# Router logits with tokens on the partitions: the normed rows as stationary operand, eight output columns, four PSUM banks

## The reference

```python
def moe_swiglu(x, w_router, w_gu, w_down):
    logits = jnp.einsum('bsd,de->bse', x, w_router).astype(jnp.float32)
    top_val, top_idx = lax.top_k(logits, TOP_K)
    gates = jax.nn.softmax(top_val, axis=-1)
    ...
    for e in range(N_EXPERTS):
        out = out + gate_full[..., e:e + 1] * swiglu(x, w_gu[e], w_down[e])
```

## Time and profile before

| what | value |
|---|---|
| median of 3 runs | 1290.58 us (1287.37 to 1291.31) |
| the profiled execution | 1289.33 us |
| its span, first to last instruction | 1287.5 us |
| PE busy | 1231.6 us, 96% of the span |
| DVE busy | 657.5 us, 51% |
| ACT busy | 538.9 us, 42% |
| mean granted PE clock | 0.987 of full speed |
| DMA | 174.10 MB, mean 135 GB/s |

### The profile page before, as it was taken

One profiled execution on the slowest core, in us unless ns is written; L12 is line 12 of the kernel. 1 busy time (PEld: TensorE's weight loads), 2 busy tenths in 40 slices (PEclk: granted clock), 3 DMA queues, 4 the chain that ended last, 5 costly groups with the idle time before them and its releaser, 6 DMA issues.

```text
span 1287.5 us, 16720 instructions
## 1 busy us (share of the span) xinstructions
PE 1231.6 (96%) x6081; PEld 1030.7 (80%) x6082; DVE 657.5 (51%) x863; ACT 538.9 (42%) x723; POOL 55.7 (4%) x67
## 2 busy tenths in 40 slices
PE   7999999999999999999999999999979999999678
PEld 6889998688888888888688789987668788877567
DVE  5333454743333333333763345534676676677774
ACT  3225541453222232213532223422576666676642
POOL 1000000000000000000000000000001312121000
PEclk9999999999999999999999999999989999999979
DMA  7331112323333333333135644122399796799751
GB/s 198 96 94 58 50 50 77 103 82 98 98 98 98 98 115 114 90 90 94 40 112 85 63 98 60 41 83 72 107 322 303 232 347 219 235 321 320 272 225 51
DMA packets 199013, 174.10 MB, mean 135 GB/s; under 512 B 7600, under 2 KB 163312, under 8 KB 198960
## 3 DMA queue, kind: packets, MB, share of 16 engines
q1 hardware_dynamic: 195264, 160.01, 42.9%
q0 software_dynamic: 3120, 11.27, 2.3%
q10 hardware_dynamic: 576, 2.10, 0.4%
HBM read 164.19 MB, written 9.18 MB: 135 GB/s over the span
## 4 chain that ended last, share of the span: by engine, by line
PE 86%; DVE 5%; DMA 3%; issue 3%; ACT 2%; ACTq 0%; SPq 0%; POOLq 0%; DVEq 0%
PE bank L792 26%; PE bank L793 25%; PE bank L794 25%; DMA raw<-moe_w_down 2%; PE bank L1184 2%; PE bank L1183 2%; DVE w_lo L1829 2%; DVE x_exact L1829 1%; PE bank L1159 1%; PE bank L1225 1%; ACT w_hi L1682 1%; PE bank L1111 1%; PE bank L885 0%; PE bank L970 0%; PE bank L930 0%
## 5 line engine op out<-in xcount | busy, mean ns | idle before, releaser
L1829 DVE TENSOR_TENSOR w_lo<-raw,w_hi 128x1024 fp32r<-128x1024 f32 (+4 forms) x206 | 285.5, 1396 | 167.4 <-ACT w_hi L1364 118.4
L792 PE MATMUL bank<-x_hi,w_hi 128*128 128x512 f32 x600 | 235.2, 392 | 3.5 <-DVE w_lo L1829 3.3
L793 PE MATMUL bank<-x_lo,w_hi 128*128 128x512 f32 x600 | 234.0, 390 | 0.0
L794 PE MATMUL bank<-x_hi,w_lo 128*128 128x512 f32 x600 | 233.9, 390 | 0.0
L1364 ACT CAST w_hi<-raw 128x1024 fp32r<-128x1024 f32 (+2 forms) x131 | 141.2, 1078 | 202.0 <-PE bank L794 202.0
L792 PE MATMUL bank<-w_hi,x_hi 128*128 128x256 f32 (+2 forms) x448 | 147.6, 329 | 7.6 <-DVE w_lo L1829 3.9
L793 PE MATMUL bank<-w_lo,x_hi 128*128 128x256 f32 (+2 forms) x448 | 145.1, 324 | 0.0
L794 PE MATMUL bank<-w_hi,x_lo 128*128 128x256 f32 (+2 forms) x448 | 144.9, 323 | 0.0
L792 PEld LDWEIGHTS bank<-x_hi,w_hi 128*128 128x128 f32 x600 | 113.0, 188 | 28.4 <-DVE w_lo L1829 4.4
L794 PEld LDWEIGHTS bank<-x_hi,w_lo 128*128 128x128 f32 x600 | 112.9, 188 | 23.7
L793 PEld LDWEIGHTS bank<-x_lo,w_hi 128*128 128x128 f32 x600 | 113.1, 188 | 23.0
(11 more groups left out here) (375 smaller groups left out, 2007.9 us busy)
## 6 DMA issues: line engine op xcount, KB each, us to landing
raw<-ffn_w_gu SPq DMA_DIRECT2D x44, 512.0 KB, 3.8
raw<-moe_w_gu SPq DMA_DIRECT2D x24, 768.0 KB, 8.5
raw<-a_w_qkv SPq DMA_DIRECT2D x24, 512.0 KB, 3.7
raw<-moe_w_gu SPq DMA_DIRECT2D x32, 384.0 KB, 6.5
raw<-moe_w_down SPq DMA_DIRECT2D x16, 768.0 KB
raw<-ffn_w_down SPq DMA_DIRECT2D x16, 704.0 KB, 4.4
raw<-kvf_w SPq DMA_DIRECT2D x16, 512.0 KB, 5.5
ring<-moe_w_down SPq DMA_DIRECT2D x16, 512.0 KB, 7.8
```

What stands on the lines that cost most here:

```text
L792: pe.matmul(o, s_hi, m_hi, start=start, stop=False, skip_group_check=True)
L793: pe.matmul(o, s_hi, m_lo, start=False, stop=False, skip_group_check=True)
L794: return pe.matmul(o, s_lo, m_hi, start=False, stop=stop, skip_group_check=True)
L1829: return dve.tensor_tensor(dst, a, b, ALU.subtract)
```

## The change

The operands of the router's matmul change places. For each k and each of the four token tiles t, a block of 128 tokens of `x_exact` (128 x 128) is the stationary operand and `w_r[:, k, :]` (8 columns) moves. The four results, 128 tokens x 8 experts each, lie in banks 4 to 7. They need no transpose: DVE copies each to its place in `logits`. The tile `logits_e`, its copy, the four transposes and the semaphore `logits_turned` go. `route_step` counts two more, and those who wait for it are adjusted.

```diff
-        logits_e = at("logits_e", [NE, SEQ], F32, G + 94 * KB)
...
             for k in range(KD):
                 pe.wait_ge(affine, 2 * KD + k + 1)
-                mm = pe.matmul(bank[5][0:NE, :], w_r[:, k, :], x_exact[:, k, :], start=k == 0, stop=k == KD - 1)
+                for t in range(TT):
+                    mm = pe.matmul(bank[4 + t][:, 0:NE], x_exact[:, k, t * P:(t + 1) * P], w_r[:, k, :],
+                                   start=k == 0, stop=k == KD - 1)
             mm.then_inc(router_done, 1)
...
-            pe.wait_ge(route_step, 1)
-            for t in range(TT):
-                mm = pe.transpose(bank[6][:, t * NE:(t + 1) * NE], logits_e[:, t * P:(t + 1) * P], ident[0:NE, 0:NE])
-            mm.then_inc(logits_turned, 1)
             turn_rows(0)
             turn_rows(1)
 
-            pe.wait_ge(route_step, 8)
+            pe.wait_ge(route_step, 10)
...
-            act.wait_ge(route_step, 4)
+            act.wait_ge(route_step, 6)
...
             dve.wait_ge(router_done, 1)
-            dve.tensor_copy(logits_e[:, :], bank[5][0:NE, :]).then_inc(route_step, 1)
-            dve.wait_ge(logits_turned, 1)
-            dve.tensor_copy(logits[:, :, :], bank[6][:, 0:TT * NE].rearrange("p (t e) -> p t e", e=NE)).then_inc(route_step, 1)
-            dve.wait_ge(route_step, 2)
             for t in range(TT):
+                dve.tensor_copy(logits[:, t, :], bank[4 + t][:, 0:NE]).then_inc(route_step, 1)
+            for t in range(TT):
+                dve.wait_ge(route_step, t + 1)
                 op = dve.max(top[:, t, :], logits[:, t, :])
             op.then_inc(route_step, 1)
```

More of the change, by code:

```diff
@@ L461, in build @@
         router_done = sem("router_done")
-        logits_turned = sem("logits_turned")
         route_step = sem("route_step")
@@ L2174, in _ @@
             dve.wait_ge(router_done, 1)
-            dve.tensor_copy(logits_e[:, :], bank[5][0:NE, :]).then_inc(route_step, 1)
-            dve.wait_ge(logits_turned, 1)
-            dve.tensor_copy(logits[:, :, :], bank[6][:, 0:TT * NE].rearrange("p (t e) -> p t e", e=NE)).then_inc(route_step, 1)
-            dve.wait_ge(route_step, 2)
             for t in range(TT):
+                dve.tensor_copy(logits[:, t, :], bank[4 + t][:, 0:NE]).then_inc(route_step, 1)
+            for t in range(TT):
+                dve.wait_ge(route_step, t + 1)
                 op = dve.max(top[:, t, :], logits[:, t, :])
             op.then_inc(route_step, 1)
-            dve.wait_ge(route_step, 3)
+            dve.wait_ge(route_step, 5)
             minus(g_diff[:, :], top[:, :, 1], top[:, :, 0]).then_inc(route_step, 1)
@@ L2186, in _ @@
             op.then_inc(route_step, 1)
-            dve.wait_ge(route_step, 5)
+            dve.wait_ge(route_step, 7)
             dve.tensor_copy(top_f[:, :, :], top_at[:, :, 0:2]).then_inc(route_step, 1)
-            dve.wait_ge(route_step, 6)
+            dve.wait_ge(route_step, 8)
             for c in range(2):
@@ L2193, in _ @@
             op.then_inc(route_step, 1)
-            dve.wait_ge(route_step, 7)
+            dve.wait_ge(route_step, 9)
             dve.tensor_tensor(sel_any[:, 0:TT, :], sel[:, 0, :, :], sel[:, 1, :, :], ALU.add).then_inc(route_step, 1)
```

## The result

| | before | after |
|---|---|---|
| median | 1286.85 us (20 runs) | 1290.01 us (20 runs) |
| range | 1284.23 to 1291.6 | 1286.22 to 1293.45 |
| span of the profiled execution | 1287.5 us | 1287.1 us |

The ratio is 1.0021, with a 95% interval of 1.0012 to 1.0031: by it the changed kernel is 2.7 us slower (1.5 to 4.0; the medians differ by 3.2), which is clear of no change but under the 0.3% that I had taken as the border. The two profiled spans do not show the loss at all. The reason comes further down: what follows the first expert's weight transfer varies by 4 us between executions, whatever the kernel. What the change does must be read from its own stretch.

The account below looks back on a forecast made before the run. PE was taken as the bound, busy 1231.6 of 1287.5 us. A list 2.1 us late gave 1291.4 from the profiled execution's 1289.33, or 1292.7 from the median; forecast 1292.0, range 1288.0 to 1297.5.

Parts of the forecast that it names:

- The router at full clock: Router matmuls on PE: 64 records at 0.117 us, 7.5 us plus 0.25 for the last result, 0.7 us longer than before.
- The handover: From the router's logits to MAX8 on DVE: four copies out of PSUM, 0.45 us against 1.43, 0.98 us saved.
- The clock falls in the router: PE's clock goes to half about 3.6 us into the router, records then 0.213 us apart; router ends at 920.1.
- The row transposes off the thread: PE's row transposes after the router start earlier and end long before DVE's sel_any, so they delay nothing.
- The sum: From router to end of list: counts 3.9 us late at 925.65, list at 931.9, so 2.1 us late.
- The clock back by the counts, DVE sets the list: After the counting matmuls: full clock on PE again, DVE's 5.64 us of tables set the list at 931.9; chance 0.45.
- The slow rival: Half clock from router to list: row transposes, embed_rows(1) and list cost 3.9 to 7.8 us, 1293.2 to 1298.4; chance 0.24.
- Do transposes count for the clock?: Row transposes on PE, 920.1 to 923.5: taken to bring the clock back; if not, time near the upper end, 7.8 us late.
- The rival of the swallowed delay: At the first expert, its 12.53 us wait for a weight transfer hides the late start: 1290.6 us; chance 0.06.

Follow-up runs that it names:

- 128-column run: Changed kernel with w_r streamed 16 times over, so each router matmul moves 128 columns and not 8: 0.9993 of the kernel before, median 1285.8 us.
- first profile with 64 columns: Changed kernel with w_r streamed 8 times over, so each router matmul moves 64 columns; first of two profiles: ratio 0.9991 to the kernel before.
- run with a known delay: Kernel before with three idle 512-column matmuls on PE ahead of the router: ratio 1.0018, 2.3 us slower (0.9 to 3.7).
- kernels with the clock kept: Changed kernel with 64 router columns (0.9991 of the kernel before), with 128 (0.9993), and with 128 plus five idle matmuls before the counts (0.9990).
- 8 and 32: Router columns per matmul: 8 is the changed kernel (1.0021 of the kernel before), 32 is it with w_r streamed 4 times over (1.0019).

## Why the prediction was right, and where it was not

- **The router at full clock: right.** 7.5 us from 0.117 for each record and 0.25 for the last result make 7.75; the 128-column run shows 7.43 with its result. No profile has the 8-column router at full clock to its end, but its records before the fall start about as far apart, (914.0 - 909.6) / 39 = 0.11 us.
- **The handover: right.** 0.45 us was forecast; 0.34 (919.31 to 919.65) and 0.40 (916.82 to 917.22) were measured. Router and handover together take 917.22 - 909.39 = 7.83 us with 128 columns, against 917.70 - 909.22 = 8.48 before. So at full clock the idea gains 0.65 us in the profiles and not 0.3.
- **The clock falls in the router: right.** Forecast 3.6 us in, seen 4.6 and 2.1 us in. The router's records at half clock in the second profile (shortest, median and longest in ns, first and last start):

```profile
L1110 PE MATMUL bank<-w_r,x_exact x46: 292/361/363, 911.5 to 921.0; 128*128 128x8 f32 x46
```

They start (921.0 - 911.5) / 45 = 0.21 us apart, for which I had taken 0.213: the load-bound spacing follows the clock in full. Columns / 1.2 ns, which the Trainium skill ("TensorE: Matmul & The Clock Gate", "LDWEIGHTS (loading the stationary operand)") gives for a load without regard to the clock, would be 0.107; the trace comes near it at full clock only.
- **The row transposes off the thread: wrong.** The prediction let them end long before `sel_any`. At half clock they take 3.51 us, in both profiles they stand in the chain, and in the first PE reaches the counts 0.2 us after `sel_any` (922.61 against 922.39). The sum was at odds with itself here: it had PE at the transposes until 923.5 and at the counts from 923.35.
- **The clock back by the counts, DVE sets the list: the step that failed** in the first profile. The row transposes between router and counts (919.2 to 922.6) did not bring the clock back; it came at 927.9, 3.1 us after the counts. PE then set the list again, 932.72 - 924.75 = 7.97 us after the counts, where I had 6.25. What made up for it was a shorter router (9.67 against 10.9). In the second profile the router took longer than forecast (11.93), but the clock was back by 925.2, and the list followed the counts by 932.48 - 926.10 = 6.38 us, as forecast. Both routes end in the same place, 23.1 us, against the 22.7 of the sum. The slow rival's mechanism was thus half there, its price was not. That the sum came so near in the first profile is two errors that cancel.
- **Do transposes count for the clock?** The Trainium skill, on the same page ("Part 4: PE-mode transpose"), holds that they do not. The traces here speak against it. The changed kernel's first profile at the place where the clock came back, at 927.9:

```profile
924.61 3.53 PE L1121 MATMUL bank<-ident,x_exact 128*128 128x128 f32 x16
927.89 0.36 PE L790 MATMUL bank<-w_hi,pt_hi 128*128 128x256 f32 x1
```

For the 3.3 us before that, PE had started nothing but row transposes. The first profile with 64 columns shows it again: half clock from 921.2, transposes from 921.2 to 924.4, full clock from 924.6. The same transposes at 919.2 to 922.6, between the 8-column router and the counts, left the clock at half. Why one stretch of them was enough and the other was not, no run here separates.
- **The base was one profile.** The sum of 2.1 us compared with a list at 20.56 us. Two of three profiles of the kernel before have 18.95, so against them the list is 4.1 us late. The measured 2.7 us lies between these two differences, 2.5 and 4.1.
- **The number: partly luck.** 1292.0 against 1290.01 looks near. But the level for the kernel before, 1290.58 from three runs, was 3.7 us above the 1286.85 of twenty, and the step put on it, 1.4 us, was 1.7 below the 3.2 by which the medians differ. The sum's own 2.1 us, on the level of twenty runs, would have given 1289.0.
- **The rival of the swallowed delay (chance 0.06): refuted** by the run with a known delay.

That the kernels with the clock kept are faster than the one before is not shown: each of their three intervals ends at 1.0000 or 1.0004. The 0.65 us that the profiles show would be a ratio of 0.9995. The 64- and the 128-column router do remove all of the change's loss.

## What to carry to other kernels

Swapping operands so that few columns move turns column time into load time. On the same path it can also take the clock away, which then slows what comes behind as well: here 13.7 us at half clock, where the router at full clock takes 7.4. PE's busy share shows nothing of it; read the granted clock in windows. Here the loads set the pace, so wider moving operands, even copies of the same columns, cost nothing (0.11 us a record with 8, 64 and 128 columns at full clock), and 64 and 128 columns kept the clock that 8 and 32 had lost.

## What the runs showed that I had not expected

- The half clock of the changed kernel lasted 13.7 us in both profiles (914.2 to 927.9, 911.5 to 925.2), through a first block of dense row transposes.
- The rest of the kernel scatters by itself, by more than the change is worth. From the weight transfer after the first split to the end it takes 1287.5 - 942.63 = 344.9 us in the kernel before and 1287.1 - 945.56 = 341.5 in the changed one, whose code there is the same. Over all fourteen profiles it lies between 341.4 and 345.5. The granted clock goes with it: in the nine profiles with 341.4 to 342.6 it held from 950 to 1210, in the five with 343.2 to 345.5 it was once at half for 3.4 us, at some place between 1169 and 1206. The two kernels' first profiles (kernel before at its fall, changed kernel over the whole stretch):

```profile
1171.40:1174.80 3.40, 3.29 (x12) 3.30 (x13) 2.51 (x4) 1.96 (x2) 0.00 (x0) 0.50 1.07 301
```

```profile
950.00:1210.00 260.00, 247.88 (x1201) 207.86 (x1199) 189.92 (x166) 174.26 (x194) 46.98 (x37) 1.00 0.89 295
```

No run was made to cause or prevent that fall, so this is a reading of fourteen profiles and not an experiment. It is why two spans tell nothing about a change of 3 us, and why I compared the stretch itself and many runs.
